# Masking the second half of the pad products straight from PSUM, ahead of the first turn, in a hybrid RWKV-7 and attention layer

## The reference

```
def step(S, inp):
    r_t, w_t, k_t, v_t, kk_t, b_t = inp
    sa = jnp.einsum('bhvk,bhk->bhv', S, -kk_t)
    S = S * w_t[:, :, None, :] + sa[..., None] * b_t[:, :, None, :] + v_t[..., None] * k_t[:, :, None, :]
    y = jnp.einsum('bhvk,bhk->bhv', S, r_t)
    return S, y
```

## Time and profile before

| | us |
|---|---|
| median of 3 runs | 1312.15 (1312.03 to 1312.87) |
| the profiled execution's own time | 1311.93 |
| its span | 1310.1 |
| TensorE busy | 1274.5 |
| VectorE busy | 722.6 |
| ScalarE busy | 698.0 |
| GpSimd busy | 307.0 |

### The profile page before, as it was taken

How to read it: one execution, slowest core, us unless ns; L and a number is a source line. 1 busy time by engine, 2 the same in 40 slices (tenths; PEclk the granted TensorE clock), 3 DMA queues, 4 the chain that set the end, 5 groups by cost and what they waited for, 6 DMA issues and landing times.

```text
span 1310.1 us, 24491 instructions
## 1 busy us (share of the span) xinstructions
PE 1274.5 (97%) x9477; PEld 1108.3 (85%) x9477; DVE 722.6 (55%) x1679; ACT 698.0 (53%) x1683; POOL 307.0 (23%) x234
## 2 busy tenths in 40 slices
PE   7999999999999999999999999999999999999996
PEld 7989798897988989798797878888888988788885
DVE  6355867768686786867765534334443434630013
ACT  6446667666676656767655634444443444542321
POOL 2430000010000100000000443334433434444443
PEclk9999999999999999999999999999999999999999
DMA  6322121212212121121222222222222222236333
GB/s 227 92 65 67 49 60 50 67 50 58 59 50 66 43 60 57 51 59 54 61 58 66 83 79 66 72 74 81 73 74 81 72 81 74 73 108 233 96 96 144
DMA packets 151523, 102.35 MB, mean 78 GB/s; under 512 B 6414, under 2 KB 140912, under 8 KB 149872
## 3 DMA queue, kind: packets, MB, share of 16 engines
q1 hardware_dynamic: 151232, 100.74, 25.7%
q10 hardware_dynamic: 176, 0.05, 0.0%
HBM read 96.57 MB, written 4.19 MB: 77 GB/s over the span
## 4 chain that ended last, share of the span: by engine, by line
PE 80%; DVE 8%; ACT 6%; issue 3%; DMA 1%; POOL 1%; SPq 0%; DVEq 0%; ACTq 0%
PE tile L593 47%; PE tile L882 2%; PE tile L884 2%; PE tile L883 2%; PE ma L852 2%; PE ma L718 1%; PE mb L867 1%; PE mb L802 1%; PE ma L727 1%; PE ma L882 1%; PE ma L884 1%; PE ma L883 1%; PE mb L882 1%; PE mb L884 1%; PE mb L883 1%
## 5 line engine op out<-in xcount | busy, mean ns | idle before, releaser
L593 PE MATMUL tile<-hn_hi,w_hi 128*128 128x264 f32 (+2 forms) x1664 | 435.1, 324 | 0.0
L593 PE MATMUL tile<-hn_hi,w_lo 128*128 128x264 f32 (+2 forms) x1664 | 429.0, 320 | 0.0
L593 PE MATMUL tile<-hn_lo,w_hi 128*128 128x264 f32 (+2 forms) x1664 | 426.5, 319 | 0.0
L1319 POOL TENSOR_TENSOR w_lo<-w_raw,w_hi 128x512 fp32r<-128x512 f32 x196 | 258.9, 1325 | 409.0 <-ACT w_hi L981 408.9
L593 PEld LDWEIGHTS tile<-hn_hi,w_hi 128*128 128x128 f32 x1664 | 270.6, 189 | 25.8 <-issue 11.3
L593 PEld LDWEIGHTS tile<-hn_hi,w_lo 128*128 128x128 f32 x1664 | 270.0, 189 | 13.6 <-issue 1.7
L981 ACT CAST w_hi<-w_raw 128x512 fp32r<-128x512 f32 x324 | 199.3, 616 | 151.0 <-PE tile L593 57.6
L593 PEld LDWEIGHTS tile<-hn_lo,w_hi 128*128 128x128 f32 x1664 | 269.9, 189 | 9.9 <-issue 0.2
L1334 POOL TENSOR_TENSOR arena<-arena,power 128x10 f32<-128x10 f32 (+3 forms) x28 | 44.2, 1579 | 575.5 <-DVE arena L1524 443.6
L1165 ACT ACTIVATE arena<-ma 64x192 f16<-64x192 f32 x240 | 77.9, 325 | 56.1 <-PE ma L718 54.7
L1174 ACT ACTIVATE arena<-ma 128x384 f16<-128x384 f32 x120 | 58.8, 490 | 68.5 <-PE ma L759 67.5
(11 more groups left out here) (259 smaller groups left out, 2161.5 us busy)
## 6 DMA issues: line engine op xcount, KB each, us to landing
w_raw<-w_in SPq DMA_DIRECT2D x260, 256.0 KB, 2.9
w_raw<-w_out SPq DMA_DIRECT2D x64, 256.0 KB, 3.0
big<-x SPq DMA_DIRECT2D x4, 1024.0 KB, 8.7
arena<-x SPq DMA_DIRECT2D x4, 1024.0 KB, 8.6
out<-big SPq DMA_DIRECT2D x3, 1024.0 KB, 3.9
arena<-post_norm_w SPq DMA_DIRECT2D x1, 1024.0 KB, 4.9
out<-big SPq DMA_DIRECT2D x2, 512.0 KB, 3.2
arena<-table_rope SPq DMA_DIRECT2D x2, 264.0 KB, 2.7
```

The costliest lines, as they stand in the source:

```text
L593: last = mm(o[:, at:at + n], w[:, slot, cols], t[:, kt, tok:tok + n], start=(kt == 0 and w is w_hi and t is hn_hi), stop=(kt == KT - 1 and ...
L1319: T(w_lo[:, slot, :], w_raw[:, slot, :], w_hi[:, slot, :].bitcast(F32), ALU.subtract).then_inc(s("lo_done"), 1)
```

## The change

ScalarE's two copies and the two later masks in place are taken out. VectorE masks the second half of the products straight from `ma` into `ar`, right behind level 0 and ahead of level 1, lower partitions first, and raises `k_masked` for each. TensorE waits for `k_masked` in the place of `kb_copied` before the first turn.

```
@@ inv_pe
                 yield inv_at(g, TURN_AT)
-                pe.wait_ge(s("kb_copied"), n)
+                pe.wait_ge(s("k_masked"), 2 * n)
                 pe.wait_ge(s("first_made"), n)
@@ inv_act
-                yield inv_at(g, 0.5)
-                act.wait_ge(s("ab_done"), n)
-                for h, rows in enumerate(halves):
-                    other = halves[1 - h]
-                    src = ma[other, h * 512:h * 512 + W].rearrange("p (c k t) -> p c k t", c=GC, k=2)
-                    last = A(ar5[other, g * GC:(g + 1) * GC, :, h, :], src, ACT.Copy)
-                last.then_inc(s("kb_copied"), 1)
@@ inv_dve
                 level(0, g3(xt16)).then_inc(s("first_made"), 1)
+                for h, rows in enumerate(halves[::-1]):
+                    masked(ar5[rows, g * GC:(g + 1) * GC, :, h, :], rows, h).then_inc(s("k_masked"), 1)
                 yield inv_at(g, LEVEL_1)
                 level(1, l4[:, 0]).then_inc(s("level_made"), 1)
-                cs = slice(g * GC, (g + 1) * GC)
-
-                def mask_k(h):
-
-                    other = halves[1 - h]
-                    m = c32[other, at:at + 2 * CH].rearrange("p (k t) -> p k t", k=2)
-                    corner = ar5[other, cs, :, h, :]
-                    TT(corner, corner, m.unsqueeze(1).broadcast_to([HD, GC, 2, CH]), ALU.mult).then_inc(s("k_masked"), 1)
-
@@ inv_dve, in the loop over the levels
-                    if l in MASK_AFTER:
-                        yield level_at(g, l, 1.4)
-                        dve.wait_ge(s("kb_copied"), n)
-                        mask_k(MASK_AFTER.index(l))
```

More of the change, by code:

```diff
@@ L314, in hybrid_layer @@
         LEVEL_1 = 1.6
-        MASK_AFTER = (2, 3)
         LAST_COLS = [[slice(0, D)]] * 3 + [[slice(0, D // 2), slice(D // 2, D)]]
```

## The result

The changed kernel takes 1330.72 us (median of 3, 1330.36 to 1330.78) against 1312.15: the ratio is 1.0137, with an interval of 1.0123 to 1.0151. The profiled execution took 1330.36 us with a span of 1328.5, so its span grew by 18.4 us.

The account below looks back on a forecast made before the run. TensorE, busy 1274.5 of 1310.1 us, bounds the kernel. 17 groups at 1.16 us (19.7) plus seven at 0.35 (2.45) less 1.4 give 20.8 on 1311.93; with 0.22 for the median, 1332.8 us, range 1326 to 1338.

Parts of the forecast that it names:

- No cover at the turn: At L734, 17 of 24 groups start 0.15 or 0.16 us after level 0, without slack; seven have 0.81 us.
- The turn's price: Two masks ahead of L734 add 1.16 us in 17 groups (19.7 us) and 0.35 in seven (2.45 us).
- The page's rules: On VectorE, masks starting on other partitions are held without overlap; the skill's table gives 0.525 us per mask, rows 0.555.
- What is given back: L1708 no longer stands behind a mask, so L802's wait of 0.20 us goes in seven passes: 1.4 us.
- Their distance stays: VectorE's work behind the masks moves 1.16 us, as TensorE does in 17 groups; in seven, 0.46 us of slack remain.
- A: TensorE's later waits shrink and win back up to 8.3 us of the stall: 1325.8 us, chance 0.06.
- B: Delay reaches beyond L734, costing another 0.3 to 0.5 us in each of 24 groups: 1343.7 us, chance 0.06.
- C: TensorE's own stream place sets L734, so masks lie beside projection work and 5.6 us come back: 1306.3 us, chance 0.03.
- D: k_masked runs ahead, TensorE finds 2n reached before this group's masks, nothing blocks L734: 1312 us, chance 0.03.
- E: Each standstill of TensorE lowers the granted clock, 24 x 2.2 = 53 us on top: 1386 us, chance 0.01.

Follow-up runs that it names:

- the last run: Kernel before the change, with only the masks in place of group g=2 moved behind levels 3 and 5 instead of 2 and 3: 1308.88 us, ratio 0.9973.

## Why the prediction was right, step by step

**No cover at the turn: right.** Reading the start times and not the listed waits was what found it. All 17 groups pay in full. The seven with 0.81 us of slack pay the rest, 0.27 us each, and only start times show it.

**The turn's price: 22.15 us forecast, 20.3 measured.** The two masks took what was summed: a gap of 0.04 us, then 1.14 us for the pair instead of 1.12. The term that was off is the way from VectorE's end to the matmul. I took 0.15 us as behind level 0; behind the mask it is 0.06, for which the last section has the reason as far as it is known. So 17 x 1.09 and 7 x 0.27 stand in the place of 17 x 1.16 and 7 x 0.35.

**The page's rules.** The trace agrees with the rule of the Trainium skill ("VectorE: DVE Perf Modes", section "Two Vector instructions with no wait between them") that an operation on other partitions is held: 0.04 us of gap at 94.81, and 0.08 us of overlap between the second mask and the level-1 multiply in the first group (95.99, 95.91). Its table's 0.525 us for a mask does not hold here: L1631's 96 take 555 ns in the mean.

**What is given back: 1.4 us forecast, 3.5 measured.** The place was right, and it is the only one, as the last run shows. The size was read from the idle time of a row (0.20 us), though I had just said that such times are too small; the start times give 0.48 us, and 0.17 in the eighth pass. Both errors made the forecast too long, by 1.9 and 2.1 us. That it came within 2.1 us owes something to luck, since 1.6 us of later steps and stores, which the sum did not have, stand against them.

**"Their distance stays": nearly.** VectorE moved by 1.16 or 1.18 us and TensorE by 1.09, so the seven waits of L759 grew by 0.07 each, 0.5 us. Another 0.28 us appeared once, at L758 behind ScalarE; this step and the one of -0.28 us at L812 and L815 are absent in every run that keeps ScalarE's copies, and they cancel. The order on GpSimd, SyncE and the DMAs did not matter, as forecast.

**The rivals.** A (won back) did not come: of the waits in the passes only L802's went. B (reaching further) came with 0.8 us of the 9.6 that I had allowed. C and D are excluded by the wait at the turn in 17 groups. E is excluded here by the clock row, which keeps its 9 behind 17 standstills of 1 us; but in two of the runs above the clock did fall, three times in all, behind longer standstills of 1.6 and 2.3 us.

**What the prediction did not see** is how little hung on the wait that it was about. It would have let a reader think that TensorE's wait on k_masked is the price. Two runs show otherwise: with the masks there and no wait, +14.8 us remain (1.6 of them the clock, in the profiled execution), and with more cover at the turn +13. In g=0 and g=2 the masks stand at the start of a stretch in which VectorE is not idle until its next delivery, so that they are paid at one delivery or the next.

The errors of the later expectations have one pattern: I was right on which wait would go and wrong on where it would turn up again, in five runs at a chain step (L807 or L812). By how much an operation may be late at each of VectorE's deliveries in a pass was never listed beforehand; whether the product or a decay product could be placed without loss is left open.

## What to carry to other kernels

An operation added to a queue costs what it makes late at the next delivery that the bounding engine takes from that queue, whether or not that engine is told to wait for it; so look where the queue is idle next, not only at the wait, and place it behind the last delivery before such idle time. Here the two masks cost 18.6 us ahead of the turn, and gave 3.8 us when, in one group of three, they were moved so that none stood ahead of that chain step and the later one lay in idle time. Count the slack by start times of matmuls against their normal distance, since the listed idle time of TensorE can be zero where 0.27 us are lost and 0.20 where 0.48 are. Where one constant sets the place on two engines, move one at a time: one shared constant cost 20 us, 3 of them by the clock that fell behind the waits. And look at the clock in a run's passes before its time is put down to queues.

## What the runs showed of the hardware that was not expected

**The way from VectorE to TensorE.** From the end of a VectorE instruction to the start of the matmul that waits for it, two distances appear at the same place of the program. It is 0.15 us where the turn has two waits ahead of it and the second one is met last: in the 17 groups of the kernel before and in those of the run with the masks early and no wait for them. It is 0.06 us behind a mask, where the first of two waits is met last, whether the mask reads PSUM or SBUF. Without the second half there is one wait, and behind the very same float16 multiply the distance is 0.06 us in eight groups:

```profile
143.92 0.63 DVE L1643 TENSOR_TENSOR arena<-arena,c 128x384 f16<-128x384 f16 x2
...
144.34 0.26 PE L732 MATMUL ma<-c,arena 128*128 128x64 f16 x3
```

The first of the two multiplies takes 0.36 us, so it ends at 144.28. In the nine others without slack it is 0.07 to 0.09 us, and there the turn starts 0.13 us behind the projection matmul ahead, as it also does in the groups with slack, so TensorE's own place sets it. The kind of VectorE instruction is therefore not what makes the difference. That a second wait that is met last costs the 0.09 us agrees with all these runs; the same two waits in the other order were not tried.

**The clock behind a standstill.** The longest standstills of TensorE in the passes were followed by the lower clock in some cases and not in others: behind two of six waits of 2.3 us (the run with the turn and ScalarE's copy later), behind one of seven of 1.6 us (masks early, no wait), and behind none of the 17 of 1.0 us in the changed kernel. Each such stretch cost 1.6 us by start times. Five runs show one more, between 19 and 24 us, while the first weights come in, and there TensorE's next wait takes up 0.7 to 1.0 us of it again. What decides between equal waits was not tried.

**The masks.** They take 555 ns out of PSUM and 549 in place, so the source hardly matters for an operation of this shape.
